# Reordering the hand-written step lists of a two-block transformer kernel: TensorE's order over the middle stages, and the distances of VectorE, ScalarE and GpSimd to it

## The reference

```python
# first block
x = x + 0.5 * swiglu(rms(x), ffn1)                 # D_FF 2816
h = rms(x, mix_norm)
rq, rk, rv, rg, dq, dk, dv, mq, gates = split(h @ w_in)
ret_out  = (rms(retention(rot(rq), rot(rk), rv)) * silu(rg)) @ ret_w_o
diff_out = rms(diff_attention(rope(rms(dq)), rope(rms(dk)), dv, lam)) @ diff_w_o
mem_out  = mem_attention(rms(mq), rms(mk), mv) @ mem_w_o
x = x + (g0 * ret_out + g1 * diff_out + g2 * mem_out) @ w_out
x = rms(x + 0.5 * swiglu(rms(x), ffn2))
# second block, layer 0 (mixer_ab) and layer 1 (mixer_c)
for layer in (0, 1):
    mix = mixer_ab(rms(h)) if layer == 0 else mixer_c(rms(h))   # delta rule + mLSTM / windowed attention
    h = h + rms(mix)
    h = h + rms(square(relu(rms(h) @ w_up)) @ w_down)
    h = h + sigmoid(h @ w_ple_gate) * (p[layer] @ w_ple)
```

## Time and profile before

| | |
|---|---|
| median of three runs | 3084.56 us (3084.54 to 3086.08) |
| profiled execution: span, first to last instruction | 3080.7 us |
| TensorE busy | 3051.1 us, 99% |
| weight loads (PEld, overlap matmuls) | 2503.3 us, 81% |
| GpSimd, ScalarE, VectorE busy | 1718.0, 1253.4, 1126.3 us |
| granted TensorE clock | 1.000 |

### The profile page before, as it was taken

One profiled execution on the slowest core, in us unless ns is written; L12 is line 12 of the kernel. 1 busy time (PEld: TensorE's weight loads), 2 busy tenths in 40 slices (PEclk: granted clock), 3 DMA queues, 4 the chain that ended last, 5 costly groups with the idle time before them and its releaser, 6 DMA issues.

```text
span 3080.7 us, 40589 instructions
## 1 busy us (share of the span) xinstructions
PE 3051.1 (99%) x15246; PEld 2503.3 (81%) x15246; DVE 1126.3 (37%) x2098; ACT 1253.4 (41%) x2278; POOL 1718.0 (56%) x1358
## 2 busy tenths in 40 slices
...
DMA packets 149840, 275.24 MB, mean 89 GB/s; under 512 B 16528, under 2 KB 17808, under 8 KB 149520
## 3 DMA queue, kind: packets, MB, share of 16 engines
...
HBM read 270.50 MB, written 2.10 MB: 88 GB/s over the span
## 4 chain that ended last, share of the span: by engine, by line
PE 94%; DVE 4%; issue 1%; ACT 1%; POOL 0%; DMA 0%; SPq 0%; DVEq 0%; ACTq 0%; POOLq 0%
PE PS L835 91%; PE PS L909 2%; DVE AR L1465 1%; PE PS L902 1%; DVE PS L1465 0%; DVE TMP L1471 0%; DVE AR L1471 0%; ACT AR L2262 0%; DMA RAW<-in_wst 0%; DVE PS L1471 0%; DVE SM L1764 0%; DVE SM L1468 0%; DVE TMP L1465 0%; POOL TMP L2662 0%; SPq L2807 0%
## 5 line engine op out<-in xcount | busy, mean ns | idle before, releaser
L2662 POOL TENSOR_TENSOR WL<-RAW,WH 128x512 fp32r<-128x512 f32 x1001 | 1295.1, 1307 | 816.8 <-ACT WH L2262 816.4
L2262 ACT ACTIVATE WH<-RAW 128x512 fp32r<-128x512 f32 x1002 | 617.6, 628 | 970.7 <-PE PS L835 901.0
L835 PE MATMUL PS<-HH,WH 128*128 128x512 f32 x2264 | 893.0, 394 | 3.8 <-ACT AR L2262 2.2
L835 PE MATMUL PS<-HL,WH 128*128 128x512 f32 x2264 | 881.6, 389 | 1.0 <-DVE HL L1471 1.0
L835 PE MATMUL PS<-HH,WL 128*128 128x512 f32 x2264 | 882.4, 390 | 0.0
L835 PE MATMUL PS<-AH,WH 128*128 128x512 f32 (+1 forms) x1504 | 581.6, 387 | 2.0 <-DVE AL L1465 1.2
L835 PE MATMUL PS<-AL,WH 128*128 128x512 f32 (+1 forms) x1504 | 578.9, 385 | 2.3 <-DVE AL L1465 2.3
L835 PE MATMUL PS<-AH,WL 128*128 128x512 f32 (+1 forms) x1504 | 578.6, 385 | 0.0
L835 PEld LDWEIGHTS PS<-HH,WH 128*128 128x128 f32 x2264 | 425.3, 188 | 96.0 <-issue 5.7
L835 PEld LDWEIGHTS PS<-HH,WL 128*128 128x128 f32 x2264 | 424.9, 188 | 90.4 <-DVE WL L1465 0.4
L835 PEld LDWEIGHTS PS<-HL,WH 128*128 128x128 f32 x2264 | 425.4, 188 | 87.5 <-DVE HL L1471 2.0
...
## 6 DMA issues: line engine op xcount, KB each, us to landing
RAW<-in_wst SPq DMA_DIRECT2D x1002, 256.0 KB, 2.7
...
```

The costliest lines, as they stand in the source:

```text
L835: return e.matmul(o, l, r, start=a, stop=z, skip_group_check=True)
L2262: return e.activation(o, a, f, **kw)
L2662: return e.tensor_tensor(o, a, b, op)
```

## The change

The steps, their instructions, tiles and arithmetic stay. `ORDER` stands in another order in six of its eight stretches, which cover differential attention, memory attention, the start of the second swiglu, layer 0's mixer, the passage into `mixer_c`, and `mixer_c` itself with the start of the feed-forward behind it. `LATE` has other numbers for 517 steps on VectorE, 335 on ScalarE and 116 on GpSimd. Two lines of the table each:

```diff
-        ("f_open", 1, 0), ("wo", 5), ("f_open", 1, 1), ("wo", 6), ("wo", 7), ("f_open", 1, 2), ("f_open", 1, 3), ("f_open", 1, 4), ("fac", "nff"),
+        ("f_open", 1, 0), ("f_open", 1, 1), ("wo", 5), ("wo", 7), ("wo", 6), ("f_open", 1, 2), ("f_open", 1, 3), ("f_open", 1, 4), ("fac", "nff"),
...
-        ("m_v", 0, 2), ("gv", 1), ("m_v", 0, 6), ("fk", 0), ("m_v", 0, 7), ("fq", 0), ("c", 1, 1), ("gs",), ("c", 1, 0), ("n", 0), ("dec", 0),
+        ("m_v", 0, 6), ("c", 0, 2), ("gv", 1), ("fq", 0), ("fk", 0), ("m_v", 0, 7), ("c", 1, 1), ("gs",), ("c", 1, 0), ("n", 0), ("gr", 0),
```

More of the change, by code:

```diff
@@ L417 @@
[L417 to L428, removed]
@@ L456 @@
     [
-        ("ab_open", 0), ("f_down", 1, 5, 4), ("ab_open", 1), ("f_down", 1, 5, 5), ("f_down", 1, 5, 6), ("f_down", 1, 5, 7), ("ab_open", 2),
-        ("ab_open", 3), ("ab_open", 4), ("c", 0, 1), ("ab_open", 5), ("ab_open", 6), ("ab_open", 7), ("fac", "nfin"), ("fac", "na"), ("ab_gl",),
-        ("bc", "na"), ("m_v", 0, 0), ("m_v", 0, 3), ("m_v", 0, 4), ("gv", 0), ("ab_gt",), ("c", 0, 0), ("m_v", 0, 5), ("c", 0, 2), ("m_v", 0, 1),
[3 rows of a table removed]
-        ("m_tri", 0, 0), ("l", 1, 0, 0), ("m_sc", 0, 0), ("m_tri", 0, 1), ("m_tri", 0, 2), ("m_sc", 0, 1), ("m_sc", 0, 2), ("m_sc", 0, 3),
[5 rows of a table removed]
@@ L493 @@
-        ("hp", "nf0", 7), ("u_open", 0, 6),
+        ("ab_open", 0), ("ab_open", 1), ("f_down", 1, 5, 4), ("f_down", 1, 5, 5), ("f_down", 1, 5, 7), ("f_down", 1, 5, 6), ("ab_open", 2),
+        ("ab_open", 3), ("ab_open", 4), ("ab_open", 5), ("ab_open", 6), ("fac", "nfin"), ("fac", "na"), ("ab_open", 7), ("c", 0, 1), ("c", 0, 0),
+        ("m_v", 0, 0), ("bc", "na"), ("m_v", 0, 3), ("ab_gl",), ("m_v", 0, 4), ("m_v", 0, 5), ("gv", 0), ("m_v", 0, 1), ("ab_gt",), ("m_v", 0, 2),
[15 rows of a table added]
+        ("n", 3), ("m_og", 2), ("m_w", 2), ("m_v", 1, 4), ("kk", 3), ("fin", 1), ("kd", 2), ("m_q", 2), ("LT", 3), ("kd", 3), ("m_k", 2),
@@ new lines @@
+        ("l", 2, 0, 0), ("m_tri", 2, 3), ("l", 3, 0, 0), ("m_v", 1, 5), ("at", 3), ("m_v", 1, 6), ("m_v", 1, 7), ("l", 2, 1, 0), ("m_tri", 2, 1),
+        ("m_sc", 2, 0), ("m_tri", 2, 2), ("l", 3, 1, 0), ("m_tri", 2, 0), ("l", 2, 1, 1), ("l", 2, 1, 2), ("vb", 2), ("m_sc", 2, 1), ("m_sc", 2, 2),
[9 rows of a table added]
+        ("o_open", "w_out_ab_2", 2), ("o_open", "w_out_ab_2", 4), ("to", "nab", 1), ("fin", 3), ("to", "nab", 0), ("o_open", "w_out_ab_2", 5),
[3 rows of a table added]
+        ("grow", "nab", 2), ("grow", "nab", 3), ("grow", "nab", 4), ("hp", "nf0", 5), ("u_open", 0, 1), ("u_open", 0, 2), ("hp", "nf0", 4),
@@ L494 @@
+        ("grow", "nab", 5), ("grow", "nab", 6), ("hp", "nf0", 6), ("u_open", 0, 3), ("grow", "nab", 7), ("hp", "nf0", 7), ("u_open", 0, 4),
+        ("u_open", 0, 5), ("u_open", 0, 6),
     ],
@@ new lines @@
+        ("d_q", 7, 1): -2, ("d_v", 7): 4, ("d_sm", 6, 3): 1, ("d_sc", 6, 3): -1, ("d_f", 7): -2, ("d_rope", 7, 0): -6, ("d_wide", 7): -4,
+        ("d_rope", 7, 1): -11, ("g", 1, 6): -6, ("g", 1, 5): -3, ("d_n", 7): -2, ("d_sc", 7, 0): -2, ("d_sm", 7, 1): -1, ("d_sc", 7, 1): -2,
[10 rows of a table added]
+        ("fac", "nff"): 4, ("f_down", 1, 5, 2): 6, ("f_down", 1, 5, 3): 5, ("f_down", 1, 5, 4): 5, ("f_down", 1, 5, 5): 5, ("f_down", 1, 5, 7): 7,
[5 rows of a table added]
+        ("m_tri", 0, 3): 1, ("m_w", 1): 11, ("m_sc", 0, 2): -1, ("l", 1, 1, 2): 5, ("l", 1, 1, 1): 5, ("xs", 5): 5, ("m_tri", 0, 1): -10,
[11 rows of a table added]
```

152 lines of the change are left out of this document (82 added, 70 removed), and 246 rows, old and new, of tables (LATE, ORDER).

## The result

The changed kernel takes 3070.85 us, the median of four runs (3070.20 to 3071.43); the kernel before took 3085.32 beside it (3084.54 to 3089.35, four runs). The ratio is 0.9948, 95% interval 0.9936 to 0.996: faster by half a per cent, where 3075.1 was forecast. The traced span fell by 11.9 us, from 3080.7 to 3068.8; the median fell by 14.5.

What follows compares the result with a forecast made beforehand. TensorE bounds the kernel, with 29.6 us idle; the change acts only on its waits. Traced 6.3 + untraced 4.5 + hidden 2.0 - new waits 3.3 = 9.5 us: span 3071.2, plus 3.9 gives 3075.1 us, range 3067 to 3083.

Steps and rivals of the forecast that it cites:

- Neither sign of being wrong: Wrong if differential attention's idle time grows by more than 3 us, or layer 0's mixer still holds over 7 us.
- ("fac", "nff"): Start of second swiglu: ScalarE's last square moves ahead of a panel conversion, GpSimd's part follows; 1.42 us gained.
- ("gs",): Layer 0's mixer: VectorE's two `("fq", 0)` instructions move behind the chain, which begins 1.76 us earlier; 1.8 us gained.
- the exchange at `("bc", "nc1")`: `mixer_c` entry: the 0.78 us wait at `("sl", 1)` goes, a new 0.9 us wait comes; net loss 0.1.
- the other 10.0 us: Some twenty smaller waits in the four stretches; about 2 us stay, 4.5 us of the other 8 gained.
- hidden time: Each removed TensorE wait also gives back 0.17 us that busy time hides; 2.0 us for some 12 waits.
- new waits in the stretches counted: Differential attention, layer 0's mixer, `mixer_c`: 11 more waits with under 2.5 us cover, 0.3 us each, 3.3 us lost.
- The rest, 10.8 us: TensorE idle time outside the four stretches, said to lie where the change does not touch or at the span's ends.
- The median stands 3.9 us above the span: Whole kernel: 3.9 us added to the forecast span of 3071.2 us gives the forecast time, 3075.1 us.
- Waits only move: Rival, chance 0.22: removed waits come back a few steps on; 3082 to 3087 us, in the middle 3084.
- Slower: Rival, chance 0.11: 11 thinner covers cost 1.0 us or more each through VectorE's strict order; 3091.6 us at 1.8 each.
- More room by the share of weight loads: Rival, chance 0.05: hidden waiting of 17 us in differential attention and 9 in `mixer_c`; could reach 3059 us.

Runs made afterwards that it cites:

- e4: Kernel before with one number changed, ScalarE's part of `("wo", 7)` two places late instead of three; 3086.32 us, ratio 0.9996.
- e9: Kernel of the three mends with ten added TensorE waits on VectorE's sums, five in each swiglu; 3084.94 us.
- e5: Kernel before with one VectorE number removed, so `("fq", 0)` stands behind the gate chain; 3087.65 us, ratio 0.9998.
- The experiment on the late tiles: Changed kernel with VectorE's parts of `("mg", 2, 2)` and `("mg", 2, 3)` back at their own places; 3068.79 us, ratio 0.994.
- the first experiment: Kernel before with the new order and distances in layer 0's mixer alone; 3075.75 us, ratio 0.9963.
- e2: Kernel before with the new order and distances in window attention (`mixer_c`) and its feed-forward's entry alone; 3082.63 us, ratio 0.9985.
- e6: Kernel before with the new order and distances of the second swiglu's start alone; 3085.41 us, ratio 0.9991.
- e11: Changed kernel with the old order and distances in layer 0's mixer alone; 3080.69 us, ratio 0.9979.
- the three mends: Changed kernel with `("mg", 2, 2)`, `("mg", 2, 3)` not late on VectorE, `("so", 7)` ahead of `("sv", 0)`, `("sv", 1)` behind `("bc", "nc1")`; 3068.65 us, ratio 0.9938.
- e7: Changed kernel with `("so", 7)` put back ahead of `("sv", 0)`; 3072.15 us, ratio 0.9951.
- e8: The same kernel as the three mends, made from the changed kernel; 3068.65 us, ratio 0.9938.

## Why the prediction was right, and where it was not

**The place and the mechanism.** The effect on the traced span lies in TensorE's waits, as it said. Neither sign of being wrong came: the idle time in differential attention fell, from 2.03 to 1.16 us, and layer 0's mixer holds 0.88. The sum by its own terms, each from the idle time before TensorE's rows:

| term | forecast | measured |
|---|---|---|
| `("fac", "nff")` | 1.42 | 1.42 |
| `("gs",)` | 1.8 | 2.04 |
| `("m_v", 0, 0)` | 1.09 | 1.09 |
| `("sp", 4)`, `("o_open", "w_o_c_2", 0)` | 2.10 | 2.10 |
| the exchange at `("bc", "nc1")` | -0.1 | 0.78 - 0.66 = 0.12 |
| `("u_open", 1, 0)` | 0 | 1.41 - 0.99 = 0.42 |
| the other 10.0 us | 4.5 | 8.4 |
| hidden time | 2.0 | -0.2 |
| new waits in the stretches counted | -3.3 | -1.2 |
| `("wo", 0)` | not in the sum | -3.0 |
| span | 9.5 | 11.2 and 0.7 elsewhere |

That 9.5 came near the span's 11.9 owes something to luck: the untraced waits gave 3.9 us more and the new ones cost 2.1 less than forecast, against 3.0 lost where nothing was forecast and 2.2 of hidden time that did not come.

**Two terms had their number for other reasons than those given.** For `("fac", "nff")` the text let "GpSimd's part follow"; ScalarE's place alone gave 0.44 of 1.42 (e4), and in one of eight kernels with the new order, e9, the wait came back. For `("gs",)` the text took 1.76 us, the two instructions of `("fq", 0)`; moved alone they gave 0.84 (e5). In the changed kernel the chain began 1776.52 - 1770.51 = 6.0 us ahead of TensorE's step, against 1780.44 - 2.04 - 1776.24 = 2.2 ahead of the moment at which TensorE was ready in the kernel before. So it gained 3.8 us on TensorE and not 1.8, since more of VectorE's list than those two moved, and GpSimd was idle all through it. Which of the moves gave the rest was not separated. The chain's first and last instruction, and GpSimd's next:

```profile
1770.51 0.17 DVE L1515 TENSOR_SCALAR SC<-SC 128x16 f32<-128x16 f32 x1
...
1774.40 0.17 DVE L1515 TENSOR_SCALAR SC<-Z 128x16 f32<-128x16 f32 x1
...
1776.24 1.01 POOL L2709 TENSOR_TENSOR SM<-SM,VC 128x4 f32<-128x4 f32 x1 [11.87 <-DVE SM L1515]
```

**"Of the other 8 I take a bit over half, 4.5" was too little.** Layer 0's mixer went from 8.63 us idle to 384.23 - 383.35 = 0.88; less the two waits named, that is 4.6. `mixer_c` went from 6.73 to 2.31; less the named ones, 1.8. In differential attention all 2.03 us of old waits went.

**"11 more" thin covers at 0.3 us each** was the wrong measure. Of all of them one showed in differential attention, 1.16 us at `("d_turn", 0, 3)`, and that one only in the three kernels in which GpSimd held VectorE just ahead of it (below). A count of covers under 2.5 us says little when the work between is one VectorE instruction of 0.7 us.

**"Each wait removed also gives back the hidden 0.17 us"** was not found as a sum: +0.9 in `mixer_c`, +0.1 in the swiglu's start, nothing in the mixer of layer 0, and -1.2 in differential attention, where the stretch grew by 0.4 us though its idle time fell by 0.9. Where waits were added to dense work, the term was larger, not smaller: five waits of 3.92 us in all made the second swiglu 332.48 - 326.87 = 5.61 us longer, 0.34 hidden in each.

**"The rest, 10.8 us, lies in stretches that the change does not touch"** is the step that failed. The change moves the end of memory attention and VectorE's `("mg", 2, m)`, and the stretch behind it lost 3.0 us at `("wo", 0)`. The experiment on the late tiles shows the cause: two numbers of the table put instructions for other tiles right ahead of the last one.

**"The median stands 3.9 us above the span"** put two things together. The span and the granted clock of every run are on record, also where no trace was kept. In the 60 runs of the kernel before that stand beside the experiments, a run's time is 2.4 to 2.5 us above its own span, and the median span is 3085.0: one run of the 60, with 3080.6, is as short as the traced 3080.7. The three runs at a granted clock of 1.000 have spans of 3080.6 to 3081.6, the 36 at 0.998 have 3083.9 to 3089.3. So the prediction started from a rare run, with no half-clock stretch before the program's end, and the median run is 4.3 us longer, at a lower clock. By my estimate 0.2% of clock missing over 3085 us, 6 us, is three or four pieces of 3.41 us at half rate; at 1.6 us each they make 5 to 6 us, and the runs at 0.998 are 5.4 longer in the mean. The four runs of the changed kernel are at 0.999, with spans of 3068.4 to 3069.6 and times 1.8 to 1.9 above them. Why the part outside the span is 0.6 us smaller stays open. Of the 4.2 us by which the time came out below 3075.1, 2.4 lie in the span and the rest in this term, which was 2.0 and not 3.9.

The same explains the first experiment. The median span fell from 3085.2 to 3073.6 us on one chip, 11.6: the stretch gave 7.9, and the other 3.7 came with the clock, which was 0.998 or lower in 12 of 20 runs before and 0.999 or 1.000 in all five after. Another 0.3 lies outside the span. Where in the program those runs were at half clock is not on record, but the traced ones give a hint: of the five other kernels with the old mixer of layer 0 (e2, e4, e5, e6, e11) all but e2 have a half-clock stretch right behind `("gs",)` (e5 a second one further on), and the seven with the new mixer have none in that stretch. Old mixer: 392.04 to 394.60 us. New: 384.15 to 384.23. That the wait of 2 us at `("gs",)` is what took most of the clock is likely and not shown: e5, where it was 1.20, is as slow as the kernel before.

**"TensorE's busy time falls by one or two us"** came out at +2.0: eight matmuls at half clock are drawn 0.63 us long instead of 0.39, which adds 8 x 0.24 = 1.9.

**The rivals.** Waits only move: fallen, the 18.8 us of the four stretches became 1.16 + 0.88 + 2.31 = 4.4. Slower: fallen as a whole; two waits of that price came, 1.16 us and the 2.12 at `("wo", 0)`, which is of the kind that it named, VectorE's strict order. More room by the share of weight loads: in differential attention that share is 267.88 of 341.86 us, 78.4% against 78.6, and the version of the three mends, with one wait left there, takes 3068.65 us and not 3059. The 17 us were not found in any order tried here; that none could find them is not shown.

**In differential attention** the new order came out better or worse than the old with the same list: 340.71 to 340.77 us in four kernels, 341.81 to 341.86 in three, against 341.47 to 341.65 with the old order. VectorE's rows on `AR` in the changed kernel and in the kernel with the late tiles taken back, which is of the faster kind:

```profile
798.91 1.76 DVE L1518 SCALAR_TENSOR_TENSOR AR<-AR,SM 128x384 f32<-128x384 f32 x1
798.96 2.87 POOL L2709 TENSOR_TENSOR WL<-RAW,WH 128x512 fp32r<-128x512 f32 x2 [0.75 <-ACT WH L2309]
```

```profile
799.76 0.62 DVE L1522 SCALAR_TENSOR_TENSOR AR<-AR,SM 128x384 f32<-128x384 f32 x1
799.81 2.96 POOL L2713 TENSOR_TENSOR WL<-RAW,WH 128x512 fp32r<-128x512 f32 x2 [0.75 <-ACT WH L2313]
```

The instruction is drawn 0.05 us ahead of GpSimd's in both (1.76 us also in e7 and e8, 0.62 in e9 and e11), so two starts that near to each other go one way or the other, and 1.1 us with them. Each kernel was traced once, so how often it goes either way is not known.
